# Modulation spread over later stages, and weight tiles split in two halves

## The reference

```python
c_act, cc_act = silu(c), silu(c_ctx)                      # one vector each, 1024 long
mod, modc = c_act @ w_mod[l] + b_mod[l], cc_act @ w_mod[l] + b_mod[l]      # 6 * 1024 values
sh1, sc1, g1, sh2, sc2, g2 = split(mod, 6)
p = (rmsnorm(x, norm1_g) * (1 + sc1) + sh1) @ w_in[l] + b_in[l]            # 24 tiles of 128 columns, and 16 gate columns
y = mLSTM, gated unit and convolution of p
x = x + g1 * (y @ w_out[l])                                                # 8 tiles
x = x + g2 * swiglu(rmsnorm(x, norm2_g) * (1 + sc2) + sh2, w_gu, w_down)   # 44 tiles, and 3 parts of 8
```

## Time and profile before

| | |
|---|---|
| median of 3 runs | 2835.37 us (2829.86 to 2836.59) |
| the profiled execution | 2841.22 us, of which its span is 2839.2 us |
| TensorE busy | 2642.4 us, 93% of the span |
| GpSimd busy | 1362.3 us, 48% |
| VectorE busy | 1594.3 us, 56% |
| first matmul on `w_in` | at 113.65 us |

### The profile page before, as it was taken

One profiled execution on the slowest core, in us unless ns is written; L12 is line 12 of the kernel. 1 busy time (PEld: TensorE's weight loads), 2 busy tenths in 40 slices (PEclk: granted clock), 3 DMA queues, 4 the chain that ended last, 5 costly groups with the idle time before them and its releaser, 6 DMA issues.

```text
span 2839.2 us, 38165 instructions
## 1 busy us (share of the span) xinstructions
PE 2642.4 (93%) x14172; PEld 2177.7 (77%) x14172; DVE 1594.3 (56%) x2160; ACT 761.0 (27%) x1565; POOL 1362.3 (48%) x1014
## 2 busy tenths in 40 slices
PE   7698999799999997999889999899999999888988
PEld 7587887688888885788667878678888887666776
DVE  7897254674573766815443333445555555656855
ACT  1222444311111123134421111312222222233423
POOL 2233223355455443333457667565555554544454
PEclk9999999899999998999999999899999999999999
DMA  9211012233232321111123232333333322223221
GB/s 378 99 53 45 30 38 104 75 124 120 89 121 94 119 84 60 53 52 53 59 69 95 93 93 91 101 106 97 95 91 97 92 89 88 82 66 90 79 93 60
DMA packets 78393, 256.53 MB, mean 90 GB/s; under 512 B 9776, under 2 KB 13616, under 8 KB 77744
## 3 DMA queue, kind: packets, MB, share of 16 engines
q1 hardware_dynamic: 60416, 211.64, 22.6%
q10 hardware_dynamic: 17840, 43.03, 4.8%
HBM read 237.33 MB, written 2.10 MB: 84 GB/s over the span
## 4 chain that ended last, share of the span: by engine, by line
PE 75%; DVE 13%; ACT 4%; issue 3%; POOL 2%; DMA 2%; ACTq 0%; SPq 0%; DVEq 0%; POOLq 0%
PE PS L405 19%; PE PS L408 18%; PE PS L406 18%; PE PS L1427 3%; PE PS L1428 3%; PE PS L1429 3%; DVE AC L2140 3%; DVE cprod L2112 2%; PE PS L616 1%; PE PS L627 1%; POOL w_lo L399 1%; DMA modv<-in_wmod 1%; PE PS L1414 1%; DVE Z L2083 1%; PE PS L611 1%
## 5 line engine op out<-in xcount | busy, mean ns | idle before, releaser
L399 POOL TENSOR_TENSOR w_lo<-raw,w_hi 128x1024 fp32r<-128x1024 f32 (+1 forms) x331 | 879.6, 2657 | 27.6
L405 PE MATMUL PS<-XH,w_hi 128*128 128x512 f32 x2168 | 825.1, 381 | 51.5 <-DVE XL L2090 11.9
L406 PE MATMUL PS<-XL,w_hi 128*128 128x512 f32 x2168 | 797.1, 376 | 0.0
L394 POOL TENSOR_TENSOR word<-ones 128x1 f32<-128x1 f32 x331 | 107.1, 323 | 1396.7 <-PE PS L408 974.5
L408 PE MATMUL PS<-XH,w_lo 128*128 128x512 f32 x2168 | 747.2, 376 | 0.0
L405 PEld LDWEIGHTS PS<-XH,w_hi 128*128 128x128 f32 x2168 | 412.6, 190 | 165.8 <-issue 37.0
L406 PEld LDWEIGHTS PS<-XL,w_hi 128*128 128x128 f32 x2168 | 412.7, 190 | 75.1
L408 PEld LDWEIGHTS PS<-XH,w_lo 128*128 128x128 f32 x2168 | 382.8, 190 | 60.1
L397 POOL TENSOR_SCALAR w_hi<-raw 128x1024 fp32r<-128x1024 f32 (+1 forms) x331 | 354.8, 1072 | 0.0
L2112 DVE CUSTOM_DVE_ANT_0 cprod<-modv,cb 128x1024 f32<-128x1024 f32 x152 | 259.5, 1707 | 26.7 <-DMA modv<-in_wmod 21.6
L1427 PE MATMUL PS<-XH,w_hi 128*128 128x512 f32 (+1 forms) x640 | 236.8, 370 | 37.7 <-DVE XL L2090 37.7
(11 more groups left out here) (311 smaller groups left out, 3477.5 us busy)
## 6 DMA issues: line engine op xcount, KB each, us to landing
raw<-in_wgu SPq DMA_DIRECT2D x88, 512.0 KB, 3.4
raw<-in_wa SPq DMA_DIRECT2D x80, 512.0 KB, 3.5
raw<-in_win SPq DMA_DIRECT2D x48, 512.0 KB, 3.5
modv<-in_wmod ACTq DMA_DIRECT2D x48, 512.0 KB, 4.9
raw<-in_wdn SPq DMA_DIRECT2D x32, 512.0 KB, 3.6
modv<-in_wmod SPq DMA_DIRECT2D x28, 512.0 KB, 11.2
QS<-Z ACTq DMA_DIRECT2D x100, 128.0 KB, 3.3
modp<-in_wmod SPq DMA_DIRECT2D x20, 512.0 KB, 12.1
```

The source lines that it names most:

```text
L394: pool.tensor_tensor(word[:, 0:1], ones[:, 0:1], ones[:, 0:1], ALU.mult)
L399: pool.tensor_tensor(lo, src, hi.bitcast(FP32), ALU.subtract).then_inc(s_split, 1)
L405: pe.matmul(acc(s)[:, a:b], hi, rh[:, i, a:b], start=i == 0, stop=False)
L406: pe.matmul(acc(s)[:, a:b], hi, rl[:, i, a:b], start=False, stop=False)
```

## The change

What it does, in layer 0 unless said otherwise:

- Start: the tiles of `sc1` (8 to 15) are reduced by VectorE; those of `sh1` (0 to 7) come as rows too, and TensorE transposes each (8 transposes), ScalarE copies the result, and TensorE multiplies it (8 matmuls). SyncE loads a row for TensorE, one feature tile of `X` and a row for VectorE in turn, eight times, then the first two tiles of `w_in`. Constants have semaphores of their own; four of them (`s_const`) are loaded after later modulation tiles, and TensorE waits for them before the in projection.
- Tiles 28 to 31: by TensorE between the norm's sum and the in projection. Tiles 24 to 27: products by GpSimd after its second split, sums by ScalarE after the norm. Tiles 16 to 23: by VectorE, three after the norm, five after `gated_linear(0)`. Tiles 32 to 35: by TensorE before `sgu_mix(0)`; VectorE reads them after `SVT`, before its next taps.
- Tiles 36 to 47: loaded behind the reload of `X`, ahead of the last four tiles of `w_out`; by TensorE before, between and after the steps of `first_tiles` of the FFN. VectorE reads the last eight after its norm, before its first turn of the FFN.
- The factor 0.5 of the activation of `cb` moves into the sums (one pass of 128x2048 less), and its tanh goes in two parts.
- Layer 1 loads its first four weight tiles before it waits for the end of layer 0.
- All 331 splits go in two halves of the contraction (steps 0 to 3, 4 to 7), and `s_split` counts both. `gemm_tile` and `tile_part` wait for each half; `first_tiles`, `first_pair` and `out_steps` wait for both.

```diff
         def split_weights(pool, s, dyn=0, k=KT):
...
-            src = raw[s % RING][:, 0:k * P].rearrange("p (k c) -> p k c", c=P)
-            hi, lo = w_hi[s % 2][:, 0:k, :], w_lo[s % RING][:, 0:k, :]
-            pool.tensor_scalar(hi, src, 1.0, 0.0, ALU.mult, ALU.add).then_inc(s_hi, 1)
-            pool.wait_ge(s_hi, s + 1 + dyn)
-            pool.tensor_tensor(lo, src, hi.bitcast(FP32), ALU.subtract).then_inc(s_split, 1)
+            for half in range(2):
+                ks = slice(half * k // 2, (half + 1) * k // 2)
+                src = raw[s % RING][:, 0:k * P].rearrange("p (k c) -> p k c", c=P)[:, ks, :]
+                hi, lo = w_hi[s % 2][:, ks, :], w_lo[s % RING][:, ks, :]
+                pool.tensor_scalar(hi, src, 1.0, 0.0, ALU.mult, ALU.add).then_inc(s_hi, 1)
+                pool.wait_ge(s_hi, 2 * s + half + 1 + 2 * dyn)
+                pool.tensor_tensor(lo, src, hi.bitcast(FP32), ALU.subtract).then_inc(s_split, 1)
...
         def gemm_tile(pe, s, rh, rl, w, dyn=0, k=KT, ready=None):
...
-            pe.wait_ge(s_split, s + 1 + dyn)
+            pe.wait_ge(s_split, 2 * s + 1 + 2 * dyn)
...
             for i in range(k):
+                if i == k // 2:
+                    pe.wait_ge(s_split, 2 * s + 2 + 2 * dyn)
...
+            for k in range(KT):
+                sp.dma_start(rowp[k][:], wmod_d[0, k]).then_inc(s_modw[k], 16)
+                sp.dma_start(X[:, k], xT[:, k]).then_inc(s_xp[k], 16)
+                sp.dma_start(rowd[k][:], wmod_d[0, KT + k]).then_inc(s_mvw[k], 16)
...
+            def mod_products():
+
+                pool.wait_ge(s_mvd, KT)
+                pool.wait_ge(s_prow, 16 * 4)
+                for i in range(4):
+                    for n in range(2):
+                        pool.tensor_tensor((prod, rowq)[n][i][:], rowq[i][:], cb[:, n, :], ALU.mult).then_inc(s_mvp, 1)
...
+            def mod_sum(m, bank, col):
...
+                for k in range(KT):
+                    last = pe.matmul(PS[:, bank, col:col + 2], modt[m][:, k, :], cact[:, k, :], start=k == 0, stop=k == KT - 1)
+                last.then_inc(s_modd, 1)
...
+                if l == 0:
+                    pe.wait_ge(s_cole, 1)
+                    for i in range(4):
+                        mod_sum(T_FIRST + 4 + i, 3, 2 * i)
                 sgu_mix(l, 0)
...
+                    mod_row_transposed(0)
+                    for k in range(1, KT):
+                        mod_row_transposed(k)
+                        mod_row_sum(k - 1)
+                    mod_row_sum(KT - 1)
                 norm(2 * l, T)
+                if l == 0:
+                    for i in range(4):
+                        mod_sum(T_FIRST + i, 4, 2 * i)
+                    pe.wait_ge(s_const, 16 * 4)
                 in_projection(l)
...
+                    if p == 0 and l == 0:
+                        def gates_of_residual(i):
+                            for m in ((39, 40, 41), (42,), (43,), (44,), (45,))[i]:
...
+                        first_tiles(pe, s, XH, XL, width(l), s_xl, KT, between=gates_of_residual)
+                        for m in (46, 47):
+                            mod_sum(m, 4, 2 * (m - 40))
...
                 act.activation(wgh[:], wg[:], ACT.Copy).then_inc(s_wgh, 1)
+                if l == 0:
+                    for i in range(4):
+                        for n in range(2):
+                            act.wait_ge(s_mvp, 2 * i + n + 1)
+                            v = (prod, rowq)[n][i][:]
+                            last = act.activation(v, v, ACT.Identity, scale=0.5, accum_out=mods[0][:, 3 * KT + i, n:n + 1])
...
                 gated_linear(0)
+                if l == 0:
+                    late_rows(3, KT)
...
                 norm(2 * l + 1, l, w)
+                if l == 0:
+                    mod_read(40, MODS, 4, KT + 20).then_inc(s_mod, 1)
```

More of the change, by code:

```diff
@@ L300, in build_program @@
         s_x = sem("x_loaded")
+        s_xp = [sem(f"x_feature_tile_loaded{k}") for k in range(KT)]
+        s_c = sem("c_loaded")
+        s_id = sem("identity_loaded")
+        s_pcl = sem("columns_of_parameters_loaded")
+        s_prow = sem("mod_rows_for_pool_loaded")
+        s_mvp = sem("mod_products_made")
+        s_mva = sem("mod_products_summed")
+        s_mtr = sem("mod_rows_transposed")
+        s_mev = sem("mod_rows_transposed_evacuated")
+        s_modr = sem("mod_sums_read")
         s_par = sem("layer_parameters_loaded")
@@ L307, in build_program @@
         s_used = sem("staged_tile_used")
-        s_modw = [sem(f"mod_weights_loaded{i}") for i in range(MOD_P)]
+        s_modw = [sem(f"mod_weights_loaded{i}") for i in range(12)]
         s_mvw = [sem(f"mod_weights_loaded_for_dve{i}") for i in range(8)]
@@ L429, in first_tiles @@
             for i in range(k0, min(k1, last)):
+                if between:
+                    between(i)
                 pe.wait_ge(sem, done + i + 1)
@@ L1260, in _ @@
                         sp.dma_start(X[:], xT).then_inc(s_x, 16)
+                        for m in range(36, MODS):
+                            if m == 45:
+                                sp.wait_ge(s_y, KT)
+                            mod_chunk(m, s_modw[m - 36])
                 for p, (h0, hn) in enumerate(PARTS):
@@ L1315, in norm, with mod_row_transposed, mod_row_sum @@
                 last.then_inc(s_squ, 1)
+            def mod_sum(m, bank, col):
+                i = m - T_FIRST
+                pe.wait_ge(s_modw[i if i < KT else i - KT], 32 if i < KT else 48 if i < 2 * KT else 16)
+                for k in range(KT):
+                    last = pe.matmul(PS[:, bank, col:col + 2], modt[m][:, k, :], cact[:, k, :], start=k == 0, stop=k == KT - 1)
+                last.then_inc(s_modd, 1)
+            def mod_row_transposed(k):
+                pe.wait_ge(s_modw[k], 16)
+                if k >= 2:
+                    pe.wait_ge(s_mev, k - 1)
+                for i in range(KT):
+                    last = pe.transpose(banks(2 * (k % 2), 2 * (k % 2) + 2)[:, i * P:(i + 1) * P], rowp[k][:, i * P:(i + 1) * P], ident[:])
+                last.then_inc(s_mtr, 1)
+            def mod_row_sum(k):
+                pe.wait_ge(s_mev, k + 1)
+                if k == 0:
+                    pe.wait_ge(s_cact, 1)
+                for i in range(KT):
+                    last = pe.matmul(PS[:, 5, 2 * k:2 * k + 2], rowt[k % 2][:, i, :], cact[:, i, :], start=i == 0, stop=i == KT - 1)
+                last.then_inc(s_modd, 1)
             def transpose_tile(l, e, src, nj):
@@ L1442, in tile_part @@
                 for i in range(k0, k1):
+                    if part == 0 and i == KT // 2:
+                        pe.wait_ge(s_split, 2 * n + 2)
                     last = three(out, w_hi[n % 2][:, i, :], w_lo[n % RING][:, i, :], i, a, b, i == 0)
@@ L2159, in _ @@
             activate_c(0)
-            for g in range(MOD_V // 4):
-                mod_tiles(0, 4 * g, 0, 4 * (g % 2), g // 2 + 1, link)
+            for k in range(KT):
+                mod_row(rowd[k], (s_mvw[k], 16), KT + k, k)
             for l in range(DEPTH):
@@ L2186, in _, with late_rows @@
                 dve.tensor_tensor(wgl[:], wg[:], wgh[:].bitcast(FP32), ALU.subtract).then_inc(s_wgl, 1)
+                def late_rows(a, b):
+                    for j in range(a, b):
+                        mod_row(rowl[j % 3], (s_mvw[j], 32), 2 * KT + j, KT + j)
+                if l == 0:
+                    mod_read(T_FIRST, T_FIRST + 4, 4, KT + 4).then_inc(s_modr, 1)
+                    dve.wait_ge(s_const, 16 * 4)
+                    late_rows(0, 3)
                 def gated_linear(f):
```

215 lines of the change are left out of this document (141 added, 74 removed).

## The result

The changed kernel takes 2800.14 us (median of 4 runs, 2795.29 to 2804.58), the one before 2834.68 us beside it (4 runs). The ratio is 0.9871, interval 0.9855 to 0.9888: 1.3% faster, some 35 us. The forecast was 2830, range 2802 to 2849. The profiled execution took 2797.02 us, 3 less than the median, and that of the trace of before 2841.22 us, 6.5 more than the median beside it; so the two traces differ by 44 us, some 10 more than the medians.

The account below looks back on a forecast made before the run. TensorE, busy 93% of the span, was taken as the bound, its 197 us idle as winnable, with VectorE on the early chain. Terms -21 + 2.5 + 8 + 1.5 + 17 - 2.5 - 11 = -5.5 us gave 2830 us, range 2802 to 2849.

Parts of the forecast that it names:

- The halves: TensorE's waits for `w_lo` across the kernel: first half ready 1.9 us sooner, whole tile 0.4 later; -11 us (-14 to 0).
- The start: Layer 0 up to `forget_sums`: VectorE's norm starts 51 us earlier, part given back; `forget_sums` at 135 us for 155.67, -21.
- term (c): Before `forget_sums`: five tiles after `gated_linear(0)` take 13 us plus a split's 2.7, all on the chain; 16 us.
- (d): Old work from 133.72 to 155.67 before `forget_sums`: 21.9 us, about 5 less as two splits leave it; 17 us.
- Term (a): VectorE's norm in layer 0: it stands still while five of GpSimd's eight products run; 12 us (0 to 19).
- The low clock behind it: Behind TensorE's wait of some 20 us at `forget_sums`: the wait leaves its clock at the low level; +2.5 us.
- Sums 32 to 35: Before `sgu_mix(0)`: VectorE waits for these sums, TensorE for the taps, the old 7.5 us wait stays; +8 us (7 to 14).
- `cb`: Out projection of layer 0: the critical `cb` load may find one or two modulation tiles ahead; +1.5 us (0 to 8).
- FFN: FFN of layer 0: VectorE's turn stands behind `mod_read(40, ...)`, which waits for the last sum; +17 us (8 to 32).
- rival 2: FFN of layer 0: sums hold TensorE's clock low, +15 us more; 2845 us, 2850 with `cb` late; chance 0.2.
- Early load: Layer 1's norm: two splits no longer fall into it, 5.93 becomes 2.2, less 1.2 for delays; -2.5 us (-3.7 to 0).
- Rival 1: Start keeps more: products end before the norm or overlap better, FFN sums run at the high level; 2805 us, chance 0.31.

Follow-up runs that it names:

- the spread: The changed kernel with every split whole again, each tile awaited once (spread modulation and layer 1's early load alone): 2822.16 us, 0.9949 of the kernel before.
- the two moves: Changed kernel with sums 32 to 35 in the wait for `lf` and the read of sums 40 to 47 behind part 0's turns: 2792.62 us; repeat 2792.66.

## Why the prediction was wrong

**The halves, -11 predicted, -30 alone (some -21 on top of the spread).** This is the step that failed. The mechanism named was right, TensorE starts on the first half, and for the waits that the term counted its size was right too: "The other 11 give 12 us at most", and 12.8 us of TensorE's waits for `w_lo` went (1.7 of them the one that the prediction counted in the stage above). But the term counted these and put everything else at nothing. In the trace 11.6 us more of waiting went, for VectorE and ScalarE, the first of which GpSimd's shorter operations block for shorter stretches; the run that awaits both halves shows that this counts by itself in layer 1. And no wait was priced by what follows it: in the trace 12.5 us came from faster matmuls, though the runs leave open how much of that is in the median. The clause that GpSimd hides its 331 x 0.4 us holds for halves and fails for quarters.

**The start, -21 at `forget_sums`, measured -27.** TensorE's sums ended at 50.3 (51 predicted), VectorE's norm ran from 56.4 to 85.3 (58.6 to 88.6), the three rows to 95.5 (102.1). `gated_linear(0)` took 2.3 us, the five rows 17.6 (term (c), 16), the rest 13.2, in place of the 17 of (d) for both. No step failed; the terms were off by a few us, above all the three rows with their splits, 10.3 for 13.5. Term (a), 12 us, is 9 by the shortened products. The wait at `forget_sums`, forecast at some 20 us, is 16.1. The low clock behind it was put at 2.5 us; 2.0 show with whole splits (27.2 us at `forget_sums` are 25.2 at the gate rows behind it).

**Sums 32 to 35, +8.** They took 8.76 us and `sgu_mix(0)` lost 9.5: right. "They don't fall into the old wait of 7.5 us, which stays" is wrong: it became 3.4, so that some 4 us came back, with the slow matmuls behind it.

**`cb`, +1.5 predicted, 3.9 at the norm's sum with whole splits**: `cb` itself took 11.99 us in the changed kernel for 11.54, and the first evacuation waited longer. Small.

**FFN, +17.** The norm's sum to tile 4 cost 10.9 us in the first trace and some 20 in the second; the low clock made the difference, as rival 2 has it, but from one execution to the next, not once for all. VectorE's queue, which the prediction followed, waited 17.8 us for the last sum, but only 2 us of that reached TensorE.

**Early load, -2.5**: 4.6 us between the norm's sum and the first `XL`, 3 or less at the end.

**Sum.** Without the halves the prediction had +5.5 us; measured are -14. The difference of 19.5 is made of the start (-6), the wait for `Ug` with its clock (-7), the FFN (-3), the load (-2) and the last attention (-3), less 2 for `cb` and 1.5 for the sums: 17.5 in one trace. The halves alone were 19 us more than predicted, and 9 of their 30 overlap with the spread. Rival 1 had the sign and nearly the time (2805), for reasons of which one came true in part: the FFN's sums at the high level, in one of two traces. As for what would show it: the start and VectorE's idle time before the FFN came as said, TensorE's wait for `lf` was 16.1 us for 20, the weight loads' waits for `w_lo` fell to 14.7 of 28.9 us, not by more than half, and the 7.5 us did not stay.

By the Trainium skill, "TensorE: Matmul & The Clock Gate", Part 1, the number of slow matmuls at a start varies from run to run of one kernel. The two traces of one kernel agree: in the first, the first eight matmuls of the in projection are slow, in the second 15 and more. They show it in the middle of a kernel too, with 10 us at stake.

What stays open: which executions get the low clock in the FFN, what share of the halves' gain is pace and not waiting, why the run that awaits both halves has two groups of times, and whether the two moves win anything by themselves.

## What to carry to other kernels

When a preparation is made shorter, count not only the waits for its product but all waits for engines that it blocks; here those were nearly as much again. A short wait of TensorE in a dense stage can cost twice, by its length and by the matmuls behind it at half speed (here 2.0 + 2.3 us); as that differs between executions, it is a bound and not a term, until runs confirm it. Splitting a preparation in parts pays by the earlier first step as long as the preparing engine has room: halves everywhere, quarters in one block of this kernel and not in the other. Work with few columns placed between dense steps makes the time depend on the clock of that execution: judge such a change by many runs, look whether they fall into groups before their median is read, and read two profiles before a term is taken from one.

## What was not expected of the hardware

- A wait of 2.02 us was followed by twelve matmuls 0.43 us apart, then 0.235 again; one of 3.44 us in the attention's out projection by seven. A wait of 2.25 us was followed by fast matmuls in one execution and by slow ones in another.
- A block of 112 entries with two columns ran at a granted clock of 0.50 with TensorE busy throughout, while the same sums between dense steps ran at the high level in one execution (0.88 over 40 us) and mostly at the low one in another (0.64).
- Half a split takes 0.62 + 1.27 us, two halves 3.8; a whole one 1.07 + 2.35. Beside VectorE's work the means are 0.82 and 1.44 for halves, 1.07 and 2.66 for whole ones.
